# Attention scores of the second and third mixer as three products of high and low parts, with each unit's query parts in two homes

## The reference

```python
# differential ("d"): 4 heads, each with two sub-heads of 64; values of 128
s = jnp.einsum('bqhjd,bkhjd->bhjqk', dq, dk) * 64 ** -0.5
p = jax.nn.softmax(s, axis=-1)
a = p[:, :, 0] - lam * p[:, :, 1]
out = jnp.einsum('bhqk,bkhe->bqhe', a, dv)
# grouped ("g"): 8 query heads, 2 key heads of 64; queries and keys are normed
s = jnp.einsum('bqhgd,bkhd->bhgqk', gq, gk) * 64 ** -0.5
out = jnp.einsum('bhgqk,bkhd->bqhgd', jax.nn.softmax(s, axis=-1), gv)
```

## Time and profile before

| | us |
|---|---|
| median of 3 runs (4403.0 to 4405.48) | 4403.24 |
| the profiled execution | 4407.63 |
| its span | 4405.6 |
| mix2, differential attention, about | 1497 to 1621 |
| mix2, grouped attention, about | 1838 to 1980 |
| mix3, differential attention, about | 3278 to 3377 |
| mix3, grouped attention, about | 3538 to 3658 |

### The profile page before, as it was taken

The page is one execution under the profiler, slowest core; times in us unless marked ns, Lnnn a source line. Parts: engine busy times, 40 slices in busy tenths (PEclk is TensorE's granted clock), DMA queues, the critical chain, the costliest instruction groups (busy, mean ns, idle before and its releaser), DMA issues.

```text
span 4405.6 us, 50811 instructions
## 1 busy us (share of the span) xinstructions
PE 3956.6 (90%) x18628; PEld 3175.8 (72%) x18628; DVE 2291.0 (52%) x3495; ACT 1369.2 (31%) x1832; POOL 1346.1 (31%) x1012
## 2 busy tenths in 40 slices
PE   7999899989997979789879879999787989788999
PEld 6888676867776748558668768888674747577887
DVE  4676844146664361641682367777445353834334
ACT  3222633242224242252112331111424243225223
POOL 2444332434432103003222223322220303434443
PEclk8999999999998989899989989999998999899999
DMA  4454221233331102001111123332110201222222
GB/s 180 176 190 156 85 72 63 96 115 128 137 132 49 39 0 72 20 1 58 57 58 58 58 82 125 118 119 100 45 48 10 82 1 67 77 84 79 95 95 86
DMA packets 57219, 364.66 MB, mean 83 GB/s; under 512 B 5744, under 2 KB 12144, under 8 KB 13936
## 3 DMA queue, kind: packets, MB, share of 16 engines
q1 hardware_dynamic: 42064, 271.11, 17.5%
q10 hardware_dynamic: 15008, 91.49, 5.5%
HBM read 360.49 MB, written 2.10 MB: 82 GB/s over the span
## 4 chain that ended last, share of the span: by engine, by line
issue 66%; POOL 23%; PE 10%; DVE 0%; ACT 0%; POOLq 0%; DVEq 0%; ACTq 0%
POOL b_wlo L561 23%; PE ps L1647 3%; PE ps L1648 3%; PE ps L1649 3%; POOLq L575 0%; ACT ps L616 0%; DVE b_y L1156 0%; DVE b_x L1160 0%; PE ps L1699 0%; DVE b_y L1183 0%; PE ps L1710 0%; ACT b_whi L602 0%; POOLq L577 0%; DVE b_y L1209 0%; PE ps L1723 0%
## 5 line engine op out<-in xcount | busy, mean ns | idle before, releaser
L561 POOL TENSOR_TENSOR b_wlo<-b_raw,b_whi 128x512 fp32r<-128x512 f32 x1008 | 1345.9, 1366 | 3039.1 <-ACT b_whi L602 3039.1
L1647 PE MATMUL ps<-b_hhi,b_whi 128*128 128x512 f32 (+1 forms) x3160 | 1178.5, 373 | 69.5 <-DVE b_vp L1548 28.8
L1648 PE MATMUL ps<-b_hlo,b_whi 128*128 128x512 f32 (+1 forms) x3160 | 1163.3, 368 | 0.0
L1649 PE MATMUL ps<-b_hhi,b_wlo 128*128 128x512 f32 (+1 forms) x3160 | 1161.4, 368 | 0.0
L1647 PEld LDWEIGHTS ps<-b_hhi,b_whi 128*128 128x128 f32 x3160 | 603.5, 191 | 177.2 <-issue 57.3
L602 ACT ACTIVATE b_whi<-b_raw 128x2048 fp32r<-128x2048 f32 x252 | 480.7, 1908 | 752.4 <-PE ps L1649 744.9
L1648 PEld LDWEIGHTS ps<-b_hlo,b_whi 128*128 128x128 f32 x3160 | 603.7, 191 | 97.8 <-issue 2.2
L1649 PEld LDWEIGHTS ps<-b_hhi,b_wlo 128*128 128x128 f32 x3160 | 602.2, 191 | 99.1
L1104 DVE SCALAR_TENSOR_TENSOR b_macc<-b_mraw,b_csil,b_macc 128x256 f32<-128x256 f32 x868 | 506.0, 639 | 7.0
L1209 DVE TENSOR_TENSOR b_y<-ps,b_y 128x512 f32<-128x512 f32 x496 | 335.8, 689 | 274.7 <-PE ps L1649 274.7
L1647 PE MATMUL ps<-b_whi,b_dhi 128*128 128x512 f32 x992 | 399.7, 403 | 53.5 <-POOL b_wlo L561 29.0
(11 more groups left out here) (277 smaller groups left out, 4752.0 us busy)
## 6 DMA issues: line engine op xcount, KB each, us to landing
b_raw<-panels SPq DMA_DIRECT2D x252, 1024.0 KB, 4.8
b_mraw<-mod_panels ACTq DMA_DIRECT2D x78, 1024.0 KB, 6.7
b_y<-mod_panels ACTq DMA_DIRECT2D x3, 1024.0 KB, 15.9
b_xin<-xT SPq DMA_DIRECT2D x1, 2048.0 KB, 25.5
b_mraw<-mod_panels SPq DMA_DIRECT2D x2, 1024.0 KB, 19.0
b_rope<-rope ACTq DMA_DIRECT2D x4, 512.0 KB, 3.9
outT<-b_xout SPq DMA_DIRECT2D x4, 512.0 KB, 3.8
b_mod<-mod_panels ACTq DMA_DIRECT2D x1, 1024.0 KB, 20.9
```

The costliest lines, as they stand in the source:

```text
L561: ins = pool.tensor_tensor(wlo[:, s, c], raw[:, s, c], whi[:, s, c].bitcast(F32), ALU.subtract)
L1647: pe.matmul(out, a[0], b[0], start=first, stop=False)
L1648: pe.matmul(out, a[0], b[1], start=False, stop=False)
L1649: return pe.matmul(out, a[1], b[0], start=False, stop=last)
```

## The change

The scores are computed by `tri` from high and low parts of keys and queries, both in fp32r. The scale of 1/8 moves into the turning of the queries (a factor in two of its instructions), into ScalarE's keeping of the context columns, and for the grouped form into the norm's gain. The high parts are ScalarE copies (`key_hi`, `query_hi`), the low parts VectorE subtractions (`key_lo`, `query_lo`). The query parts have two homes, by the parity of the unit; unit n+1 is prepared at the first row of unit n. The zero halves are written once for each home (`query_masks`). The homes and some key parts lie in the weight slot that is free during an attention. The values' panels of the differential form come after the queries' panels instead of before them; TensorE waits for the values only at the first weighing.

```diff
-    ps = cols_panels(w, 0, 1024) + cols_panels(w, 1664, 2176) + merge(4480, v["w_br_diff_2"][l])
+    ps = cols_panels(w, 0, 512) + cols_panels(w, 1664, 2176) + cols_panels(w, 512, 1024) + merge(4480, v["w_br_diff_2"][l])
...
+    def last_reader(self, n, j):
+        found = [r for r in range(len(self.rows)) if self.rows[r][0] in range(n % 2, n, 2) and j in self.rows[r][2]]
         return found[-1] if found else None
+    def prepared_at(self, r):
+        n = self.rows[r][0] + 1
+        return n if self.unit_start(r) and n < len(self.units) else None
...
+    def split_keys(st, tag, t):
+        if tag == "g":
+            return whi[:, (first[st] + 16) % 2, 0:TT], gkl[:, :]
+        hi = (kh01[:, 0, :], kh01[:, 1, :], kh2[:, :], whi[:, (first[st] + 7) % 2, 0:TT])[t]
+        return hi, kl[:, t, :]
...
             # ScalarE
+            def key_hi(tag, t):
+                src = dk[:, t, :] if tag == "d" else gk[:, 0, :]
+                act.activation(split_keys(st, tag, t)[0], src, ACT.Copy).then_inc(*up("k_hi", X(tag, t)))
+            def query_hi(rows, uno):
+                t, half, g = rows.unit(uno)
+                a, b = GROUPS[g]
+                hi, _ = split_query(st, rows.tag, uno)
+                for j in rows.halves(uno):
+                    prev = rows.last_reader(uno, j)
+                    if prev is not None:
+                        act.wait_ge(*at("scores", X(rows.tag, prev, j)))
+                    else:
+                        act.wait_ge(*at("q_masks", X(rows.tag, uno % 2)))
+                    act.wait_ge(*at(*rows.query_event(X, t, g)))
+                    o = slice(64 * j, 64 * j + 64)
+                    act.activation(hi[o, j, 0:b - a], aq[o, t, a:b], ACT.Copy).then_inc(*up("q_hi", X(rows.tag, uno, j)))
...
                 for r in range(len(rows)):
                     steps = rows.next_steps(r)
+                    if rows.prepared_at(r):
+                        query_hi(rows, rows.prepared_at(r))
...
+            for t in range(3):                      # after the keys' panels
+                act.wait_ge(*at("ctx_kept", X("dk", t)))
+                key_hi("d", t)
+            # queries' panels, then query_hi(rows, 0), then values' panels
+            act.wait_ge(panel_used, panel[0])
+            act.wait_ge(*at("ctx_kept", X("dk", 3)))
+            key_hi("d", 3)
             attention(rows)
...
             # VectorE
+            def query_lo(rows, uno):
+                ...
+                for j in rows.halves(uno):
+                    o = slice(64 * j, 64 * j + 64)
+                    dve.wait_ge(*at("q_hi", X(rows.tag, uno, j)))
+                    dve.tensor_tensor(lo[o, j, 0:b - a], aq[o, t, a:b], hi[o, j, 0:b - a].bitcast(F32), ALU.subtract)\
+                       .then_inc(*up("q_lo", X(rows.tag, uno, j)))
+            def query_masks(rows, n):
+                for part in split_query(st, rows.tag, n):
+                    for half in range(2):
+                        o = slice(64 * (1 - half), 64 * (1 - half) + 64)
+                        ins = dve.tensor_copy(part[o, half, :], pr2[o, 0, 1, 0:L])
+                ins.then_inc(*up("q_masks", X(rows.tag, n)))
+                dve.wait_ge(*at("q_masks", X(rows.tag, n)))
...
             def attention(rows):
-                for r, j in rows.first_steps():
-                    if rows.unit_start(r):
-                        masked_query(rows, r, j)
+                chain(dve.memset(pr2[:, 0, 1, 0:L], 0.0))
+                if rows.tag == "g":
+                    dve.wait_ge(panel_used, p0 + 15)
+                query_masks(rows, 0)
+                if rows.tag == "g":
+                    key_lo("g", 0)
+                query_lo(rows, 0)
+                if rows.tag == "d":
+                    dve.wait_ge(panel_used, p0 + 6)
+                query_masks(rows, 1)
+                if rows.tag == "d":
+                    key_lo("d", 3)
                 for step in rows.first_steps():
                     row_max(rows, *step)
                 for r in range(len(rows)):
                     steps = rows.next_steps(r)
-                    for q, j in steps:
-                        if rows.unit_start(q):
-                            masked_query(rows, q, j)
                     row_probs(rows, r)
+                    if rows.prepared_at(r):
+                        query_lo(rows, rows.prepared_at(r))
                     for step in steps:
                         row_max(rows, *step)
...
             # TensorE, row_scores
                 if rows.unit_start(r):
-                    pe.wait_ge(*at("qm", X(rows.tag, rows.unit_no(r), j)))
+                    pe.wait_ge(*at("k_lo", X(rows.tag, u[0] if rows.tag == "d" else 0)))
+                    pe.wait_ge(*at("q_lo", X(rows.tag, rows.unit_no(r), j)))
...
-                    pe.matmul(ps[:, b, :], q, keys(u)[:, 0:L], start=True, stop=True)
-                    ins = pe.matmul(ps[:, b + 1, 0:LC], q, keys(u)[:, L:TT], start=True, stop=True)
...
+                for n, (c0, c1) in enumerate(GROUPS if k0 == 0 else GROUPS[1:]):
+                    ins = tri(ps[:, b + n, 0:c1 - c0], q, (hi[:, c0:c1], lo[:, c0:c1]), True, True)
```

More of the change, by code:

```diff
@@ L308, in bank, with halves @@
         return 2 * (j if self.tag == "d" else r % 2)
-    def last_row_with(self, n, j):
-        found = [r for r in range(len(self.rows)) if self.rows[r][0] < n and j in self.rows[r][2]]
+    def halves(self, n):
+        half = self.units[n][1]
+        return (0, 1) if half is None else (half,)
+    def last_reader(self, n, j):
+        found = [r for r in range(len(self.rows)) if self.rows[r][0] in range(n % 2, n, 2) and j in self.rows[r][2]]
         return found[-1] if found else None
+    def prepared_at(self, r):
+        n = self.rows[r][0] + 1
+        return n if self.unit_start(r) and n < len(self.units) else None
     def last_unit_of(self, t):
@@ L969, in mix2 @@
                        .then_inc(*up("ctx_kept", X("dk", 2 * a + n)))
+            for t in range(3):
+                act.wait_ge(*at("ctx_kept", X("dk", t)))
+                key_hi("d", t)
+            for a in range(2):
+                next_split()
+                for n in range(2 if T > L else 0):
+                    act.wait_ge(*at("roped", X("dq", 2 * a + n)))
+                    act.activation(aq[:, 2 * a + n, L:TT], ps[:, 2 * (2 * a + n) % 4 + 1, 0:LC], ACT.Copy, scale=SCALE)\
+                       .then_inc(*up("ctx_kept", X("dq", 2 * a + n)))
+            rows = ROWS(st, "d")
+            query_hi(rows, 0)
             for a in range(2):
@@ L1004, in mix2 @@
             rows = ROWS(st, "g")
+            act.wait_ge(panel_used, panel[0])
+            act.wait_ge(*at("roped", X("gk", 0)))
+            key_hi("g", 0)
+            query_hi(rows, 0)
             attention(rows)
@@ L1507, in mix2 @@
                 turn("dk", t, ps[:, 2 * t % 4, :], dk[:, t, 0:L], pr2[:, 1, t % 2, 0:L], "rope")
+            for t in range(3):
+                key_lo("d", t)
             for t in range(4):
-                dve.wait_ge(*at("out", (p0 + 4 + t // 2, t % 2)))
-                turn("dq", t, ps[:, 2 * t % 4, :], aq[:, t, 0:L], pr2[:, 1, t % 2, 0:L], "rope")
+                dve.wait_ge(*at("out", (p0 + 2 + t // 2, t % 2)))
+                turn("dq", t, ps[:, 2 * t % 4, :], aq[:, t, 0:L], pr2[:, 1, t % 2, 0:L], "rope", SCALE)
             for t in range(4):
@@ L1532, in mix2 @@
             for t in range(4):
[L1533 removed]
+                normed_and_turned("gq", t, GQ_BANK[t], 6, T, small[:, 50:51], aq[:, t, 0:T])
             for t in range(4):
@@ L2050, in weigh, with attention @@
                 ins.then_inc(*up("pv", X(rows.tag, uno)))
-            def attention(rows, keys, values):
+            def attention(rows, values, last_value):
                 for step in rows.first_steps():
-                    row_scores(rows, *step, keys)
+                    row_scores(rows, *step)
                 for r in range(len(rows)):
                     for step in rows.next_steps(r):
-                        row_scores(rows, *step, keys)
+                        row_scores(rows, *step)
                     if r >= 1 and rows.unit_end(r - 1):
-                        weigh(rows, r - 1, values)
+                        weigh(rows, r - 1, values, last_value)
                     u, i, js, k0, k1 = rows[r]
@@ L2066, in attention @@
                     ins.then_inc(*up("tr", X(rows.tag, r)))
-                weigh(rows, len(rows) - 1, values)
+                weigh(rows, len(rows) - 1, values, last_value)
             for a in range(2):
```

90 lines of the change are left out of this document (47 added, 43 removed).

## The result

The changed kernel takes 4425.24 us (median of 5 runs, 4423.34 to 4431.36) where the kernel before, run beside it, takes 4403.24 (5 runs, 4401.76 to 4406.1): a ratio of 1.0045, 95% interval 1.0033 to 1.0056. It is 22 us slower; the forecast was 27 us faster.

A forecast was written before the change was run, and what follows sets the result against it. TensorE, busy for 90% of the span, was taken as the bound, with VectorE its nearest rival. The terms 12+8+4+5+5-5-2 = 27 us came off the median of 4403.24 us, giving 4376 us; range 4358 to 4393.

The forecast's parts named there:

- Part 3: Differential attention of mixer three: shorter steps and scalings leaving the loop save 1.1 us a unit, 4 us; bounds 0 and 9.
- Rival (c): Preparing a unit ahead isn't covered: 72 us lost against 27 gained, 4448 us in full; chance 0.05.
- Part 1: Grouped attention of mixer three: a unit takes 12.55 us, saving 1.5; eight units save 12 us; bounds 6 and 17.
- Part 2: Grouped attention of mixer two: 1.0 of 1.75 us saved per pair of units, 8 us; bounds 4 and 14.
- Part 4: Differential attention of mixer two: 1.2 us saved in each of four pairs, 5 us; bounds 0 and 10.
- Part 5: Start of the differential attentions: values' panels last save net 2.5 us each, 5 us for both; bounds 0 and 12.
- Part 6: Start of the grouped attentions: added preparation loses 2.7 us each, 5 us for both; bounds 3 and 8.
- Part 7: Panels of mixer three: key copies ahead of the split delay the next query panel, loss 2 us; bounds 0 and 4.
- rival (b): Three-part products gain little because new weights come every 256 columns; mostly waits go, 15 us, 4388 us; chance 0.07.
- rival (a): Clock falls in each differential unit, costing about 20 us and leaving 7 us gained, 4396 us; chance 0.16.

The follow-up runs named there:

- run 1: Changed kernel, with query parts for the unit behind each two-row unit of mixer two prepared one row earlier: 4404.27 us, 0.999 of the kernel before.
- run 2: Changed kernel, with TensorE issuing the previous unit's weighing ahead of the score steps in a two-row unit's first row: 4405.04 us, 0.9993 of the kernel before.
- run 10: Changed kernel, with GpSimd making both query parts from unit two on, other engines' order and starts kept: 4403.04 us, 0.9986 of the kernel before.
- run 7: run 5 with only 8 columns of each query copied and subtracted from a home's second use on (wrong scores): 4385.56 us, 0.9956 of the kernel before.
- run 3: Changed kernel, with low query parts behind two-row units computed for 8 columns instead of 512: 4416.45 us, 1.002 of the kernel before.
- run 4: Changed kernel, with the copies of the keys' high parts moved behind the next panel's split on ScalarE: 4429.66 us, 1.0049 of the kernel before.
- run 5: Changed kernel, with the earlier preparation of run 1 in the grouped attentions alone: 4399.76 us, 0.9983 of the kernel before.
- run 8: run 5 with ScalarE writing the grouped starts' zeros and VectorE subtracting the key's low part while awaiting a root: 4394.43 us, 0.9968 of the kernel before.
- run 12: Kernel before, with only the panel order changed, queries' panels ahead of values' in mixers two and three: 4393.01 us, 0.9962 of the kernel before.
- run 6: run 5 with one full-precision product of the high parts in place of three products, preparation kept: 4412.12 us, 1.0007 of the kernel before.
- run 9: run 8 with GpSimd making both parts of each query from unit two on: 4395.68 us, 0.9968 of the kernel before.

## Why the prediction was wrong

**The failed step** stands in Part 3: preparation is "both issued at the unit's first row. There the weighing of the unit before covers them". That needs the weighing to stand ahead of the step that reads the new query. In four-row units it does. In a two-row unit TensorE's own order puts the next unit's first step ahead of it, in the same row in which the query is prepared. I had listed TensorE's order as steps, weighing, transposes, and knew the lead of two rows, but looked at how long the cover is and not at what stands behind what. Rival (c), preparation not covered, was priced for all 36 units and dismissed by "24 of the 36 units start beneath a weighing of 5.15 us". It happened behind seven of the eight two-row units of mix2's grouped attention, at 4.3 us each in place of 1.5: the wait alone is 2.7, because the copy stands behind two other ScalarE instructions, and the low clock comes on top. That is 30 us. Runs 1, 2 and 10 each take 20 us or more off. In mix2's differential attention the same step failed three times, at 2.0 us of wait; there run 1 took the wait away and gained nothing.

**Part 1** (-12): the unit is 12.97, not 12.55 us, against 14.15 before on the mean, not 14.09; without the start, mix3's grouped attention gained 8.6. **Part 2** (-8): with the order repaired +2. Run 7 puts 7 us of the gap on the load, 0.95 us in each of seven intervals; the rest I put down to the loop, which no run takes apart further. **Part 3** (-4): the intervals as predicted, 1.2 us in each of the first two (the third, 18.57 before, only 0.3); over the whole attention the splits show 2.6 in the changed kernel and 0.5 to 1.3 in runs 1 to 5 and 8, which are written alike there. **Part 4** (-5): -1.2 in the changed kernel, within that attention's own spread. **Part 5** (-5): -3.4 up to mix2's first steps and -3.5 behind mix3's query panels, where 2.5 each was said; run 12 shows that the panel order alone gives 3.6 and 5.5. **Part 6** (+5): TensorE's wait grew from 18.3 to 20.2 and from 14.9 to 17.1 us, +4.1. The 2.6 us that the working gives for it don't come out of its own terms (3.5 less 1.4 is 2.1), and the subtraction of the key's low part (0.96 us, run 8's expectation) is missing in them. **Part 7** (+2): 3.0 us of wait at mix3's second query panel, where it was looked for; run 12, without the key copies, has 0.4.

Beside the failed step one term was mis-sized, and it is not the products. Of the 29 us in Parts 1 to 4 the working gives 12 to them (rival (b) is what is left without them: 15 of 27), and run 6 measures 12. The other 17 were the queries leaving the units' loops (6+5+3+3). With the order repaired and the starts set apart, run 6 has for these four terms -3, +7, +2 and 0: +6 in place of -17. A copy and a subtraction of 0.6 and 0.7 us for one scaling of 0.4 are still on the two engines that set the length of a row, and run 7 prices them at 14 us, all but 2 or 3 of them in mix2. In mix3, where every unit has a long weighing over its preparation, taking them out leaves the units as they are. The two errors, 26 us of order and 23 of queries, come to 49 us, the distance from -27 to +22. But the splits of the changed kernel's profile account for 40 of it only (-27 to +13), so this agreement doesn't prove that nothing else is missing.

Of rival (a) the mechanism is real, but its place was wrong: the clock falls in the grouped attention of mix2 in the 2.8 us waits, and in mix3's differential one it went up (0.93 to 0.95).

**What stays open:** what decides whether mix2's differential attention runs at a clock of 0.90 or 0.98 in kernels that are written alike there; and some 9 of the 22 us by the medians, which the splits, read in one execution, don't place (they place 13).

## What to carry to other kernels

Work prepared a unit ahead is covered only if the long instruction stands in the consumer's queue ahead of the first one that reads it; write out the order for the *shortest* unit, where the lead reaches over the whole of it. A wait taken away counts only if none stands right behind it, as in the differential attention of run 1. Change the order of independent transfers or projections first: here one swap, which puts the late vector work of the queries beneath the values, gave 17 us by the medians (9 of them placed at the two starts) and needed no new work. And count the preparation that a shorter product needs as load on the engines of the loop, even where it is issued early: here it cost 14 us where the products gave 12, nearly all of it where no long weighing lay over it.

## What the hardware showed that I had not expected

- GpSimd and VectorE hold one another up in some of their instructions, and nearly exclude one another there. A scaling of 128x768 takes 0.62 us alone and 1.42 when it starts 0.30 us into a GpSimd subtraction of 1.29 (run 9): 0.80 us more, of the 0.99 that the subtraction still lasts. A maximum read from PSUM takes its 0.96 us beside GpSimd's copy and the start of that subtraction (same rows). GpSimd's four subtractions of a panel took 7.17 us instead of 5.05 beside VectorE's, and VectorE's three 5.36 instead of 2.69 (run 4). The Trainium skill, "SBUF — State Buffer", "SBUF: two separate sides", calls the pair of ports that the two share an exclusive lock, held for the whole instruction, which VectorE takes in certain instructions alone; the rows of run 9 agree, but for the last 0.19 us.
- A wait of 2.8 us costs more than itself: the granted clock falls to 0.50 within it, and the weighing behind it took 6.91 us at first and 5.9 to 7.4 in the following pairs, instead of 5.31.
